# Every RMS norm of a two-layer trunk: VectorE adds one half of the squared planes onto the other, and TensorE sums four planes in place of eight

## What is computed

```python
def rms_norm(x, w):
    y = xf * lax.rsqrt(jnp.mean(xf * xf, axis=-1, keepdims=True) + EPS)
    return (y * w).astype(x.dtype)

for i in range(DEPTH):                                  # 2 layers
    hn = rms_norm(h, norm_mix_pre[i])
    m = deltanet_stickbreak_mixer(hn, ...) if i % 2 == 0 else s5_mixer(hn, ...)
    h = h + rms_norm(m, norm_mix_post[i])
    hn = rms_norm(h, norm_ffn_pre[i])
    f = swiglu_ffn(hn, ffn_w_gate[i], ffn_w_up[i], ffn_w_down[i])
    h = h + rms_norm(f, norm_ffn_post[i])
```

## Time and profile before

| | us |
|---|---|
| median of three runs | 3039.7 |
| lowest and highest | 3034.1 and 3047.1 |
| the profiled execution, whole | 3037.27 |
| its span in the profile | 3035.5 |
| PE busy in the span | 2799.8 |
| DVE busy | 1223.2 |
| ACT busy | 616.8 |
| POOL busy | 953.6 |

### The profile page before, as it was taken

The page is one execution under the profiler, slowest core; times in us unless marked ns, Lnnn a source line. Parts: engine busy times, 40 slices in busy tenths (PEclk is TensorE's granted clock), DMA queues, the critical chain, the costliest instruction groups (busy, mean ns, idle before and its releaser), DMA issues.

```text
span 3035.5 us, 45389 instructions
## 1 busy us (share of the span) xinstructions
PE 2799.8 (92%) x18337; PEld 2668.2 (88%) x18337; DVE 1223.2 (40%) x2148; ACT 616.8 (20%) x1093; POOL 953.6 (31%) x390
## 2 busy tenths in 40 slices
PE   7999978889999999999999885569999999999997
PEld 7999957767889999999999784459989999999996
DVE  4655057755244444444423612620242333222234
ACT  4221133345242001011001420220240000000002
POOL 4444300000343433333343222005234443443330
PEclk7999989889999999999999987779999999999998
DMA  4232511110221222222231336952122111111102
GB/s 133 87 119 91 123 56 43 33 61 28 80 98 50 79 78 71 71 71 71 71 109 42 94 80 148 228 129 70 34 98 87 49 55 41 42 55 42 42 28 74
DMA packets 173101, 232.51 MB, mean 77 GB/s; under 512 B 59456, under 2 KB 138560, under 8 KB 170816
## 3 DMA queue, kind: packets, MB, share of 16 engines
q1 hardware_dynamic: 69680, 137.25, 15.9%
q10 hardware_dynamic: 103312, 93.71, 10.0%
HBM read 170.89 MB, written 60.03 MB: 76 GB/s over the span
## 4 chain that ended last, share of the span: by engine, by line
PE 36%; issue 34%; POOL 14%; DMA 6%; DVE 5%; ACT 2%; ACTq 1%; SPq 1%; POOLq 0%; DVEq 0%
POOL w_hi L645 9%; PE psum L673 8%; PE psum L674 8%; PE psum L675 8%; POOL w_lo L649 5%; DMA stage<-wstream 4%; PE psum L733 2%; PE psum L1093 2%; PE psum L1065 1%; DMA area<-s_u 1%; PE psum L1161 1%; PE psum L1080 1%; PE psum L928 1%; PE psum L949 1%; DVE area L1908 1%
## 5 line engine op out<-in xcount | busy, mean ns | idle before, releaser
L673 PE MATMUL psum<-x_hi,w_hi 128*128 128x344 f32 (+2 forms) x3600 | 1170.5, 325 | 46.9 <-DVE x_lo L1932 25.0
L674 PE MATMUL psum<-x_lo,w_hi 128*128 128x344 f32 (+2 forms) x3600 | 1165.0, 324 | 0.0
L675 PE MATMUL psum<-x_hi,w_lo 128*128 128x344 f32 (+2 forms) x3600 | 1160.4, 322 | 0.0
L645 POOL TENSOR_TENSOR w_hi<-stage,const 128x1024 fp32r<-128x1024 f32 x193 | 480.1, 2487 | 1982.2 <-PE psum L675 1955.6
L673 PEld LDWEIGHTS psum<-x_hi,w_hi 128*128 128x128 f32 x3600 | 687.6, 191 | 52.6 <-DVE x_lo L1932 21.6
L674 PEld LDWEIGHTS psum<-x_lo,w_hi 128*128 128x128 f32 x3600 | 686.6, 191 | 1.8
L675 PEld LDWEIGHTS psum<-x_hi,w_lo 128*128 128x128 f32 x3600 | 687.4, 191 | 0.0
L649 POOL TENSOR_TENSOR w_lo<-stage,w_hi 128x1024 fp32r<-128x1024 f32 x193 | 477.7, 2475 | 15.1
L673 PE MATMUL psum<-act_hi,w_hi 128*128 128x344 f32 (+1 forms) x1056 | 346.0, 328 | 18.5 <-DVE area L2399 13.1
L675 PE MATMUL psum<-act_hi,w_lo 128*128 128x344 f32 (+1 forms) x1056 | 340.7, 323 | 0.0
L674 PE MATMUL psum<-act_lo,w_hi 128*128 128x344 f32 (+1 forms) x1056 | 339.7, 322 | 0.0
(11 more groups left out here) (221 smaller groups left out, 2118.5 us busy)
## 6 DMA issues: line engine op xcount, KB each, us to landing
stage<-wstream SPq DMA_DIRECT2D x193, 512.0 KB, 3.6
s_set<-area ACTq DMA_DIRECT2D x8, 1860.0 KB, 8.2
proj<-area ACTq DMA_DIRECT2D x28, 520.0 KB, 2.6
area<-proj ACTq DMA_DIRECT2D x36, 256.0 KB, 3.5
resid<-area ACTq DMA_DIRECT2D x6, 1376.0 KB, 5.7
area<-resid ACTq DMA_DIRECT2D x6, 1376.0 KB, 8.5
area<-proj ACTq DMA_DIRECT2D x12, 520.0 KB, 5.5
area<-s SPq DMA_DIRECT2D x4, 1348.0 KB, 7.9
```

Of the source, the lines that this page charges most:

```text
L645: pool.tensor_tensor(per_block(w_hi[:, slot, :]), per_block(stage[:, h, :]), all_ones, ALU.mult).then_inc(high_split, 1)
L673: mm(out[:, 0:n], w_hi[:, slot, wk], hi[:, xk, a:a + n], start=first, stop=False)
L674: mm(out[:, 0:n], w_hi[:, slot, wk], lo[:, xk, a:a + n], start=False, stop=False)
L675: return mm(out[:, 0:n], w_lo[:, slot, wk], hi[:, xk, a:a + n], start=False, stop=last)
```

## The change

PE no longer sums 8 planes, of which 4 are the first half and 4 the second. A new DVE function norm_pair waits for both halves of the squares, adds the second half (4 planes) onto the first in one instruction and raises nm_paired; PE waits for that and sums 4 planes. ACT's instructions and their order stay as they were.

```diff
@@ PE, norm_sum @@
-                for k in range(KT):
-                    if k % 4 == 0:
-
-                        pe.wait_ge(nm_square, 2 * e + k // 4 + 1)
-                    last = mm(sums[:, 0:n], ones, sq[k // 4][:, k % 4, 0:n], start=(k == 0), stop=(k == KT - 1))
+                pe.wait_ge(nm_paired, e + 1)
+                for k in range(KT // 2):
+                    last = mm(sums[:, 0:n], ones, sq[0][:, k, 0:n], start=(k == 0), stop=(k == KT // 2 - 1))
                 last.then_inc(nm_sum, 1)
@@ DVE @@
+            def norm_pair(r, c, m):
+
+                n = CUTS[c][1]
+                e = norm_event(r, c, m)
+                low, high = first_sq[c] if r == 0 else sq_halves
+                dve.wait_ge(nm_square, 2 * e + 2)
+                V.tensor_tensor(low[:, :, 0:n], low[:, :, 0:n], high[:, :, 0:n], add).then_inc(nm_paired, 1)
+
-            def norm_post(r, c):
+            def norm_post(r, c, paired=False):
 
                 a, n = CUTS[c]
+                if not paired:
+                    norm_pair(r, c, 0)
                 h, rr = nv["h"][c % 2][:, :, 0:n], norm_scale(r, c, 0)
...
             def norm_pre(r, c):
 
                 n = CUTS[c][1]
+                if r:
+                    norm_pair(r, c, 1)
                 h, rr = first_h[c] if r == 0 else nv["h"][c % 2], norm_scale(r, c, 1)
@@ DVE, at the start @@
+            norm_pair(0, 0, 1)
+            norm_pair(0, 1, 1)
             norm_pre(0, 0)
+            norm_pair(0, 2, 1)
             norm_pre(0, 1)
@@ DVE, at the end of an FFN @@
                 norm_low(r + 1, 0)
+                norm_pair(r + 1, 1, 0)
                 add_down(end, 2)
-                norm_post(r + 1, 1)
+                norm_post(r + 1, 1, True)
```

More of the change, by code:

```diff
@@ L426, in trunk @@
         nm_square = sem("nm_square")
+        nm_paired = sem("nm_paired")
         nm_log = sem("nm_log")
```

## The result

| | before | changed |
|---|---|---|
| median, us | 3040.8 (4 runs) | 3102.8 (4 runs) |
| lowest and highest | 3034.1, 3047.1 | 3098.8, 3107.8 |
| profiled execution, its span | 3037.3, 3035.5 | 3102.5, 3100.7 |
| granted clock, mean of the span | 0.955 | 0.937 |

The changed kernel is slower: the ratio is 1.0205, with an interval of 1.0178 to 1.0232. That is 62 us where 37 were predicted; the direction was right, and the time is outside the range (3055 to 3090).

The account below looks back on a forecast made before the run. TensorE, busy 92% of the span, looked like the bound, but waits for the add would outweigh savings: +16.7 us net plus 20 for lost clock, 37 in all, giving 3077 us, range 3055 to 3090.

Parts of the forecast that it names:

- (a): Sums (1, 0, post) and (2, 2, pre): add done long before TensorE arrives; together -4.7 us.
- rival 2: Seams of rounds 1 to 4: adds done before TensorE arrives, 48.9 us saved, 2992 us; chance 0.05.
- (b): Four pre sums whose squares end just in time, VectorE free: waits of 1.2 to 1.5, together -4.0 us.
- (c): Six sums whose add stands behind a step fed by TensorE's product just before the sum: together +9.7 us without clock.
- (d): Sums (1, 1, post), (1, 2, post), (3, 2, post), add behind a long low part: together +8.6 us without clock.
- (e): Sum (2, 1, post), the dearest: wait of 12.3 us, partly replacing later waits; net +4.7 us without clock.
- (f): Sums (2, 0, pre), (2, 1, pre), (2, 2, post), (3, 0, post), (4, 2, post): together +0.8 us without clock.
- (g): Kernel's start: the third cut's add stands between two scalings ahead of the low part; +1.6 us, other bound +2.1.
- the price of the clock: Half clock behind long waits: 12 places at 1.5 us plus three counted half, +20 us, bounds 0 and 25.
- the add's price beside GpSimd: Each of the 24 new VectorE adds taken as 1.6 us, with 2.8 as the bound.
- The main case: Waits for the adds and lost clock together make the kernel slower, 3077 us (3065 to 3085); chance 0.67.
- rival 3: Adds beside GpSimd's splits take 2.8 us, not 1.6, at some eight places: 10 us more, 3087; chance 0.09.

Follow-up runs that it names:

- Experiment 5: Changed kernel with 12 of its 24 adds placed earlier in VectorE's row; 3041.4 us against 3040.6 for the kernel before, ratio 1.0006.
- experiment 2: Changed kernel with TensorE multiplying planes of a constant in the idle time before 19 sums; 3068.3 us, ratio 1.0074 to the kernel before.
- experiment 7: Changed kernel with the add kept at 15 of 24 sums, 11 moved early, eight planes at the rest; 3025.5 us against 3040.6, ratio 0.9951.
- experiment 9: Kernel of experiment 7 with GpSimd splitting only 128 of every 1024 columns from the first FFN on; 2995.8 us, ratio 0.9865 to the kernel before.
- experiment 4: Changed kernel with GpSimd splitting only 128 of every 1024 columns from the first FFN on; 3062.3 us, ratio 1.0046 to the kernel before.

## Why the prediction was right or wrong

Waits in this section count, as in the prediction, from the time at which the sum could have started; that is 0.16 more than the idle time in the timeline.

**Right: the place of the add decides.** The 21 sums behind the start came with waits before 19 of them, and the two of (a) had none. Experiment 5 confirms it by time: other places for the same 24 adds, and 61 of 62 us are gone. The page's occupancy, by which TensorE is the engine to relieve (the rule of the Trainium skill that stood as rival 2, "Perfetto Trace Analysis", Identifying the Most-Contended Engine), gave no hint of this; the trace sided with the rows of the seams.

**Right: what halving is worth.** 48.9 reckoned, 41.5 measured without the add, with 35 to 49 as the interval.

**The terms one by one.** For each sum I took from both traces how much later TensorE arrives and how much later the sum ends; the difference is its net. The prediction's column has its clock prices put where it counted them (six places of c, three of d, e, two and three halves of f):

| term | predicted, clock included | measured |
|---|---|---|
| (a) two sums done early | -4.7 | -4.7 |
| (b) four sums, squares just in time | -4.0 | +6.7 |
| (c) six behind a step on TensorE's own product | 9.7 + 9 = 18.7 | +19.8 |
| (d) three behind a low part | 8.6 + 4.5 = 13.1 | +14.4 |
| (e) sum (2, 1, post), to the end of the down | 4.7 + 1.5 = 6.2 | +9.5 |
| (f) five others | 0.8 + 5 = 5.8 | +10.9 |
| (g) the start | 1.6 | +1.8 |
| between the sums | 0 | +6.8 |
| together | 36.7 | 65.2 (the two spans) |

Of the last but one row 3.2 lie in the products right behind the sums; the rest is drift of both signs (+2.8 before round 1, -3.1 in the first FFN, +3.3 in the S5 part, +0.7 in the second FFN), which no run here explains and which is within what executions of one kernel differ by. That (c) and (d) come out so near is in part luck. In (d), sum (1, 1, post) cost 5.5 where 1.2 + 1.5 stood, but (1, 2, post) and (3, 2, post) cost 4.0 and 4.9 where 3.7 + 1.5 stood for each. In (c), (3, 1, post) cost 5.5 as well, while (1, 2, pre) kept its clock and cost 1.6.

**Wrong, first: the price of the clock.** The prediction read a stretch of 3.0 us at half rate, took half of it, 1.5, and counted 12 places and three halves. It lost the clock at 16 of the 21, and each cost 2.2 on the mean (34.5 / 16). The single place bears this out: 4.21 against 2.10 at sum (1, 1, post) is 2.1 in the sum alone, and at (1, 1, pre) 4.8 us of the stretch lie on work. So the term was mis-sized by some 15 us, and its stated upper bound of 25 was too low.

Both the count and the price were off. Of the twelve places (1, 2, pre) kept the clock; the three short waits that I had counted by half all lost it, and so did (1, 1, pre) and (3, 1, pre), which I hadn't counted. The price of 1.5 came from a window of 3.0 inside one stretch. The windows of the changed kernel show how much of a stretch falls on work: the first two lie in the wait before (1, 1, pre) and behind that sum (the row on the sum itself stands in the section on the result), the other three on (2, 0, post) and behind it:

```profile
899.80:901.80 2.00, 0.00 (x0) 0.00 (x0) 1.95 (x1) 0.22 (x1) 1.92 (x2) 0.50 1.03 248
906.70:910.00 3.30, 3.30 (x23) 3.30 (x22) 2.18 (x5) 0.96 (x2) 2.02 (x1) 1.00 0.12 19
...
1680.70:1681.40 0.70, 0.70 (x3) 0.49 (x4) 0.00 (x0) 0.00 (x0) 0.00 (x0) 1.00 0.00 0
1681.50:1684.80 3.30, 3.30 (x8) 1.78 (x7) 0.00 (x0) 0.00 (x0) 0.00 (x0) 0.50 0.02 5
1684.90:1688.00 3.10, 3.10 (x22) 3.10 (x20) 1.94 (x4) 2.26 (x3) 0.00 (x0) 1.00 0.00 0
```

At (2, 0, post) and six more sums the half clock began only with the sum or up to 1 us into it, and 3.4 us of it fell on work, a loss of 1.7. At the other nine it had begun during the wait and lasted longer: 3.8 to 5.5 us of it fell on the sum and the products behind it, a loss of 1.9 to 2.7. Half of this time over all 16 places is 33.4 us, which agrees with the 34.5 of experiment 2.

**Wrong, second: the add's price beside GpSimd.** 1.6 was taken and 2.8 put as the bound; seven adds took 2.40, 3.72, 3.35, 2.58, 3.72, 3.30 and 3.33, together 11 us more than seven of 1.6. With the clock this is most of (b)'s miss: sums (1, 1, pre) and (3, 1, pre) waited 4.1 and 4.4 in place of 1.5 and lost the clock; their nets went from about -1 to +4.0 and +4.3. The miss of 3.3 at (e) is the long add, 2.1, and the longer stretch at half clock, 1.2.

The step that failed was to take 1.6 for every add, since L1913's mean left no room for longer ones, and to read L1932's 5.31 as a factor of 1.75 for the bound. It is not a factor. In the rows of the changed kernel shown above the low part, the add and the splits take turns: L650, from 875.23, ends at 880.30; the add, from 878.03, ends at 881.75, 1.45 after that; L646, from 880.27, ends at 883.96, 2.2 after the add's end. Experiment 5's rows have the same pattern, at 881.43 and 882.89. All seven long adds of the changed kernel came while a split was running, and all seven ended 1.45 to 1.48 after that split's end; none of the 17 adds of 1.6 had a split beside it. So the add waits for the end of the running split and then takes nearly its own time, and the price is additive: up to a whole split (2.4) on top of 1.6, so 4.0. The Trainium skill says this too ("SBUF — State Buffer", 🔬 SBUF: two separate sides): the port pair that VectorE and GpSimd share is locked for a whole instruction, not split, and the loser is fully blocked. These rows agree with it, and by it the bound would have been 4.0.

**Wrong, third: rivals that exclude each other.** The main case at 3077 and rival 3 at 3087 were given chances as alternatives, but both mechanisms act in the same run. Rival 3 reckoned 10 us at eight places with 1.2 each; it was 11 at seven places with 1.6 on the mean. Predicted 37, plus 14.5 of clock, plus 11 of adds comes to 62; that it meets the measured 62 so closely is in part luck, since the interval is 8 us on either side and smaller terms moved both ways. A second reckoning agrees: with the clock's loss filled away (experiment 2) 27.5 us remain by the medians (22.5 by the ratio), where the prediction's sum without the clock was 16.7 and the adds took 11 more.

**Smaller points.** At (1, 2, post) the wait was 4.1 and not 6.0, since the low part ran without GpSimd this time (3.02 in place of 4.90); at (3, 2, post) it was 5.2. For (e) the wait was 14.4 where 12.3 stood, by the long add. The waits of the 21 sums come to 85 us against 70 predicted. Of the signs to look for, the halved group, the falling busy time, the waits ended by the add and their longest place came true. Three did not: seven adds were not of 1.6; the longest waits after that of (2, 1, post) stood at (1, 1, post) and (3, 1, post), with 5.7, and not at (1, 2, post) and (3, 2, post); and behind the wait of 3.8 at (1, 2, pre) the clock stayed at 1.00, as the window at 946.00 shows.

**Where the rest of the gain went.** Of the 35 us that fifteen halved sums could bring (15 x 2.33), 15 came. The traces of experiment 7 and of the kernel before, set beside each other at every sum, place the missing 20. Some 14 lie at the seams of rounds 1 and 3: sums (1, 1, post) and (3, 1, post) end 2.4 later in place of 2.3 earlier, and the pre sums behind them, which kept eight planes, 2.1 and 2.4 later; experiment 9 brings 10 of these 14 back by short splits. Another 3.2 lie at (1, 0, pre) and (3, 0, pre), whose squares end just in time, and 2.3 at (2, 1, post), where the wait for the weights behind the sum grows by what the sum saves (0.78 before, 3.08 in experiment 7).

**Open.** A kernel with another order for GpSimd's splits wasn't tried.

## What to carry to other kernels

Before handing a part of the busiest engine's work to an idle one, look at the seams: when does the new instruction's input arrive, what stands in front of it in that engine's row, and when does the busy engine come to the result? An idle engine with an in-order row is not idle at that spot. Where the waits come out near or above what has lost the clock elsewhere in the trace, price the lost clock by all the work that may fall into the half-clock stretch (1.7 to 2.7 us a place here), and where the trace shows two engines taking turns, add the other's whole instruction instead of scaling by a factor. Split work off only at the places where the result is ready early: all 24 lost 62 us, 15 or 13 chosen ones gained some 15.

## What the runs showed of the hardware

- VectorE's instructions with two inputs in SBUF and GpSimd's splits took turns: the add took 1.59 alone and up to 3.79 beside a split, the split 2.4 alone and up to 5.2. Cutting the splits short gave the kernel before 28 us; how much of that comes from the turns and how much from earlier weights wasn't told apart.
- Nearly the same wait kept the clock once and lost it another time. The wait at (1, 2, pre) kept it in the changed kernel. In that of experiment 4, at the same place, TensorE's timeline has

```profile
940.40 4.95 PE L733 MATMUL psum<-area,const 128*128 128x344 f32 x8 [3.67 <-DVE area L1908]
```

  and in that of experiment 5, at (3, 1, post), a wait of 2.82 kept it (2.55 for eight records), which at (1, 1, post) of the same run lost it:

```profile
2205.40 2.55 PE L742 MATMUL psum<-area,const 128*128 128x344 f32 x8 [2.82 <-DVE area L1927]
```

- Of a stretch at half clock 3.4 us fell on TensorE's work where it began on or behind the start of the sum (seven sums of the changed kernel), and 3.8 to 5.5 where it had begun in the wait (nine sums).
